# Sixteen expert products on one core: the up products split into two halves of 32 tokens, the second half behind a run-time branch

## The reference, cut to what matters

```python
scores = sigmoid(h @ w_router)
sel = scores + b_router
# the best of four groups of four experts, then the two best experts in it
_, idx = top_k(where(in_group, sel, -inf), 2)
for e in range(16):
    he = silu(h @ w1[e]) * (h @ w3[e])
    out = out + gates[:, e:e + 1] * (he @ w2[e])
```

## Time and profile before

| | us |
|---|---|
| median of 3 executions | 988.1 |
| lowest and highest | 986.34 and 995.4 |
| the profiled execution | 996.42 |
| its span in the trace | 994.6 |

### The profile page before, as it was taken

One profiled execution on the slowest core, in us unless ns is written; L12 is line 12 of the kernel. 1 busy time (PEld: TensorE's weight loads), 2 busy tenths in 40 slices (PEclk: granted clock), 3 DMA queues, 4 the chain that ended last, 5 costly groups with the idle time before them and its releaser, 6 DMA issues.

```text
span 994.6 us, 11764 instructions
## 1 busy us (share of the span) xinstructions
PE 936.2 (94%) x4268; PEld 513.5 (52%) x4269; DVE 416.4 (42%) x894; ACT 304.7 (31%) x693; POOL 31.4 (3%) x54
## 2 busy tenths in 40 slices
PE   3999999999998999987999999999989999999998
PEld 1464456565443344332455445455765546577763
DVE  1279597634461012421222322601956633336452
ACT  3200534232412213340322331312465632125420
POOL 0100200000000000000000002000000000000000
PEclk9999999999999999997999999999989999999999
DMA  9998614488559799898799999404227724423401
GB/s 350 362 386 316 141 58 173 161 318 320 204 222 337 239 360 387 299 392 318 278 396 393 397 378 307 154 31 159 87 86 252 224 74 169 169 88 111 130 13 42
DMA packets 105693, 230.74 MB, mean 232 GB/s; under 512 B 3125, under 2 KB 6505, under 8 KB 105497
## 3 DMA queue, kind: packets, MB, share of 16 engines
q1 hardware_dynamic: 100288, 217.85, 61.8%
q0 software_dynamic: 2208, 7.37, 2.6%
q10 hardware_dynamic: 3128, 4.62, 1.4%
HBM read 224.31 MB, written 5.51 MB: 231 GB/s over the span
## 4 chain that ended last, share of the span: by engine, by line
PE 78%; DVE 8%; DMA 6%; ACT 4%; issue 2%; SPq 1%; POOLq 1%; ACTq 0%; POOL 0%; DVEq 0%
PE bank L646 23%; PE bank L913 12%; PE bank L926 6%; PE bank L660 5%; DMA arena<-in_w_mod_dram 5%; PE bank L943 4%; PE bank L1221 3%; PE bank L1150 3%; PE bank L1240 2%; PE bank L1231 2%; PE bank L612 2%; DMA arena<-in_gla_w_in_dram 1%; PE bank L842 1%; PE bank L938 1%; PE bank L775 1%
## 5 line engine op out<-in xcount | busy, mean ns | idle before, releaser
L646 PE MATMUL bank<-arena 128*128 128x512 f32 (+3 forms) x592 | 238.0, 560 | 4.3 <-DMA arena<-in_gla_w_in_dram 2.3
L646 PEld LDWEIGHTS bank<-arena 128*128 128x128 f32 x592 | 111.8, 191 | 122.5 <-issue 110.4
L913 PE MATMUL bank<-arena 128*64 128x512 f32 x512 | 114.6, 600 | 2.9 <-issue 2.9
L660 PE MATMUL bank<-arena 128*128 128x256 f32 (+1 forms) x384 | 99.1, 416 | 2.8 <-ACT arena L1945 1.5
L660 PEld LDWEIGHTS bank<-arena 128*128 128x128 f32 x384 | 72.1, 190 | 30.6 <-issue 21.4
L913 PEld LDWEIGHTS bank<-arena 128*64 128x64 f32 x512 | 39.4, 139 | 74.5 <-issue 73.8
L926 PE MATMUL bank<-arena,con 128*64 128x512 f32 x272 | 67.7, 644 | 4.7 <-ACT con L1848 4.0
L2395 DVE TENSOR_TENSOR con<-con,bank 128x256 f32<-128x256 f32 x17 | 7.1, 420 | 111.1 <-ACT con L1753 111.1
L1749 ACT ACTIVATE con<-bank 128x256 f32<-128x256 f32 x17 | 6.5, 384 | 139.9 <-PE bank L913 139.9
L926 PEld LDWEIGHTS bank<-arena,con 128*64 128x64 f32 x272 | 22.3, 147 | 39.7 <-issue 38.6
L612 PE MATMUL bank<-arena,silu_c 128*32 128x512 f32 x272 | 35.9, 652 | 5.6 <-DMA arena<-in_w_mod_dram 4.1
(11 more groups left out here) (415 smaller groups left out, 1207.1 us busy)
## 6 DMA issues: line engine op xcount, KB each, us to landing
arena<-in_w_gate_e_dram SPq DMA_DIRECT2D x16, 2048.0 KB, 14.5
arena<-in_w_up_e_dram SPq DMA_DIRECT2D x16, 2048.0 KB, 13.2
arena<-in_w_down_e_dram SPq DMA_DIRECT2D x16, 2048.0 KB, 12.8
arena<-in_w_mod_dram SPq DMA_DIRECT2D x12, 2048.0 KB, 16.4
arena<-in_mod_w_dram SPq DMA_DIRECT2D x12, 2048.0 KB, 8.2
arena<-in_ab_w_in_dram SPq DMA_DIRECT2D x7, 2048.0 KB, 9.2
arena<-in_gla_w_in_dram SPq DMA_DIRECT2D x6, 2048.0 KB, 16.2
arena<-in_cd_w_in_dram SPq DMA_DIRECT2D x6, 2048.0 KB, 7.8
```

Of the source, the lines that this page charges most:

```text
L646: mm = pe.matmul(ps[:, 0:n], lhs[:, k, tile * P:(tile + 1) * P], w[:, k, c0:c0 + n], start=(k == 0), stop=(k == kd_ - 1))
L660: mm = pe.matmul(ps[:, i * n:(i + 1) * n], w[:, k, c * P:(c + 1) * P], rhs[:, k, 0:n], start=(k == 0), stop=(k == KC - 1))
L913: mm = pe.matmul(up_b[64 * j:64 * j + 64, :], h[:, k, :], blocks[:, g + n:u + n + 1:u - g, :], start=(k == 0), stop=(k == KC - 1), tile_po ...
```

## The change

- The up products of an expert are split by tokens (`up_half`). A half is 32 tokens: for each chunk k four matmuls with 32 stationary columns and 256 moving columns, each on its own 32 columns of the array (`tile_position=(0, 32 * j)`), with a quarter of the gate and of the up weights. The first half writes columns 0 to 255 of `up_b`, the second columns 256 to 511.
- DVE computes `passes`: 0 for up to 32 tokens, 1 for 33 to 64, 2 and more beyond, in four small linked steps and a copy, ahead of `extra_flag`.
- PE reads `passes` of the expert into a register. Above 0 it takes the wide branch: the loop of three surplus rounds, which now compares this register with the round's number, and then the second half. Otherwise it raises one semaphore. The first half is computed last, after the branch, in both cases. Expert 0 always computes both halves.
- `x_up`, `x_turned` and `x_down` become one semaphore, `x_step`, with three steps per round; an idle round raises it by 3 in one instruction without drains.
- ACT and DVE read and write the same number of elements as before, in another order (`ff_halves` and the views with `a` and `g`). `down` picks its columns of `ffT` accordingly.

Lines of the diff that only rename semaphores are left out:

```diff
@@ -216,6 +217,7 @@
         small = sb("small", [P, 1024 - 256 - 96])
         route_idx = sb("route_idx", [P, TT, 2], I32)
         extra_flag = sb("extra_flag", [P, NE, EXTRA], I32)
+        passes = small[:, 352:352 + NE].bitcast(I32)
         first_slot = small[:, 288:288 + NE * (1 + EXTRA)].rearrange("p (e t) -> p e t", t=1 + EXTRA).bitcast(I32)
 
         arena = sb("arena", [P, MAIN + 6 * SLOT])
@@ -223,6 +225,7 @@
         RING = MAIN + 3 * SLOT
         SPARE = KC * (2 * T + CAP)
         blocks = arena[:, :].rearrange("p (n c) -> p n c", c=256)
+        quarters = arena[:, :].rearrange("p (n c) -> p n c", c=P)
 
         def view(off, *dims):
             n = int(np.prod(dims))
@@ -273,6 +276,7 @@
         hs = [view(12800, KC, CAP), view(13312, KC, CAP)]
         spent = con[:, cols["levels"][0]:cols["levels"][0] + 768]
         act1, act2, ffT = spent[:, 0:256], spent[:, 256:512], spent[:, 512:768].rearrange("p (c s) -> p c s", c=2)
+        ff_halves = spent[:, 512:768].rearrange("p (q a s) -> p a q s", q=4, a=2)
...
@@ -523,6 +526,15 @@
                                                         sem("cdga_ready"))
         conv_in, cd_conv = sem("conv_in"), sem("cd_conv")
         sink_exp = sem("sink_exp")
+
+        def x_upped(n):
+            return n * 3 + 4
+
+        def x_turned(n):
+            return n * 3 + 5
+
+        def x_downed(n):
+            return n * 3 + 6
 
         block = ctx.enter_context(nc.Block())
 
@@ -903,27 +915,38 @@
             def landed_expert(e, j):
                 pe.wait_ge(landed[expert_slot[e][j]], 16 * expert_fill[e, j])
 
-            def up(h, e, sem_, gathered=False):
+            def up(h, e, sem_):
                 g, u = (slot_at(s) // 256 for s in expert_slot[e][0:2])
                 for k in range(KC):
-                    if gathered:
-                        pe.wait_ge((hg_a, hg_v)[k % 2], k // 2 + 1)
                     for j in range(2):
                         n = 2 * k + j
                         mm = pe.matmul(up_b[64 * j:64 * j + 64, :], h[:, k, :], blocks[:, g + n:u + n + 1:u - g, :],
                                        start=(k == 0), stop=(k == KC - 1), tile_position=(0, 64 * j))
                 mm.then_inc(sem_, 1)
 
+            def up_half(h, half, e, gathered=False):
+                g, u = (slot_at(s) // P for s in expert_slot[e][0:2])
+                for k in range(KC):
+                    if gathered:
+                        pe.wait_ge((hg_a, hg_v)[k % 2], k // 2 + 1)
+                    for j in range(4):
+                        n = 4 * k + j
+                        mm = pe.matmul(up_b[32 * j:32 * j + 32, 256 * half:256 * half + 256],
+                                       h[:, k, HALF * half:HALF * half + HALF], quarters[:, g + n:u + n + 1:u - g, :],
+                                       start=(k == 0), stop=(k == KC - 1), tile_position=(0, 32 * j))
+                return mm
+
             def turn_ff(sem_):
                 for c in range(2):
                     mm = pe.transpose(t_b[:, c * P:(c + 1) * P], act2[:, c * P:(c + 1) * P], ident)
                 mm.then_inc(sem_, 1)
 
-            def down(e, sem_):
+            def down(e, sem_, whole):
                 w2 = view(slot_at(expert_slot[e][2]), 4, D)
                 for kc in range(4):
+                    c, at = (kc // 2, 64 * (kc % 2)) if whole else (kc % 2, 64 * (kc // 2))
                     for q in range(2):
-                        mm = pe.matmul(dn_b[64 * q:64 * q + 64, :], ffT[:, kc % 2, 64 * (kc // 2):64 * (kc // 2) + 64],
+                        mm = pe.matmul(dn_b[64 * q:64 * q + 64, :], ffT[:, c, at:at + 64],
                                        w2[:, kc, 512 * q:512 * q + 512], start=(kc == 0), stop=(kc == 3),
                                        tile_position=(0, 64 * q))
                 mm.then_inc(sem_, 1)
@@ -950,30 +973,25 @@
                 project_gates(f"ga{n}", "ab4" if c else "ab3_ctx" if half else "ab3", [2 * i, 2 * i + 1], c == 1,
                               hT_ctx if half else hT_lat, ga_copied, n + 1)
 
-            pe.sem_inc(x_up, 1)
-            flags = extra_flag[0:1, :, :].rearrange("p e t -> p (e t)")
-
-            def extras(e):
+            pe.sem_inc(x_step, 3)
+
+            def extras(e, blocks_of_e):
                 with pe.Fori(0, EXTRA) as t:
-                    n = t + e * EXTRA
-                    flag = pe.value_load(flags[:, bass.ds(n, 1)], min_val=0, max_val=1)
-                    with pe.If(flag > 0):
+                    with pe.If(blocks_of_e > t + 1):
+                        n = t + e * EXTRA
                         pe.wait_ge(x_h, n + 1)
-                        up(hs_x, e, x_up)
+                        up(hs_x, e, x_step)
                         pe.wait_ge(x_ff, n + 1)
-                        turn_ff(x_turned)
+                        turn_ff(x_step)
                         landed_expert(e, 2)
                         pe.wait_ge(x_ffT, n + 1)
-                        down(e, x_down)
+                        down(e, x_step, False)
+                        pe.drain()
                     with pe.Else():
-                        pe.drain().then_inc(x_up, 1)
-                        pe.drain().then_inc(x_turned, 1)
-                        pe.drain().then_inc(x_down, 1)
+                        pe.sem_inc(x_step, 3)
 
             def no_extras():
-                pe.sem_inc(x_up, EXTRA)
-                pe.sem_inc(x_turned, EXTRA)
-                pe.sem_inc(x_down, EXTRA)
+                pe.sem_inc(x_step, 3 * EXTRA)
 
             def ctx_turned_latents(t):
                 pe.wait_ge(c_ready, t - 1)
@@ -1090,34 +1108,37 @@
                 ctx_work(CTX_WORK_TURNED.get(e, []))
                 landed_expert(e, 2)
                 pe.wait_ge(ffT_ready, e + 1)
-                down(e, down_done)
+                down(e, down_done, True)
 
             for e in range(NE):
                 for j in range(2):
                     landed_expert(e, j)
                 if e == 0:
-                    up(hg[:, :, 0:CAP], e, up_done, True)
-                any_extra = pe.value_load(flags[:, e * EXTRA:e * EXTRA + 1], min_val=0, max_val=1)
+                    up_half(hg, 1, e, True)
+                    up_half(hg, 0, e).then_inc(up_done, 1)
+                blocks_of_e = pe.value_load(passes[0:1, e:e + 1], min_val=0, max_val=1 + EXTRA)
                 if e == 0:
-                    with pe.If(any_extra > 0):
+                    with pe.If(blocks_of_e > 1):
                         ctx_latents(6)
                         gather()
                         behind_up(e)
-                        extras(e)
+                        extras(e, blocks_of_e)
                     with pe.Else():
                         no_extras()
                         c_place[0] -= 6
                         ctx_latents(6)
                         gather(True)
                         behind_up(e)
-                    pe.wait_ge(x_down, EXTRA)
+                    pe.wait_ge(x_step, x_downed(EXTRA - 1))
                     continue
-                with pe.If(any_extra > 0):
-                    extras(e)
+                with pe.If(blocks_of_e > 0):
+                    extras(e, blocks_of_e)
+                    pe.wait_ge(hs_ready, e)
+                    up_half(hs[e % 2], 1, e)
                 with pe.Else():
                     no_extras()
                 pe.wait_ge(hs_ready, e)
-                up(hs[e % 2], e, up_done)
+                up_half(hs[e % 2], 0, e).then_inc(up_done, 1)
                 behind_up(e)
                 ctx_work(CTX_WORK_BEHIND.get(e, []))
             for i in range(3):
@@ -1399,7 +1420,7 @@
                         banks.wait(sp, "qkT311")
                     sp.wait_ge(down_done if j0 == 2 else up_done, e0 + 1)
                     if e0 == 0:
-                        sp.wait_ge(x_down if j0 == 2 else x_up, EXTRA + (0 if j0 == 2 else 1))
+                        sp.wait_ge(x_step, x_downed(EXTRA - 1) if j0 == 2 else x_upped(EXTRA - 1))
                 elif s == 0:
                     banks.wait(sp, "y01")
                 elif s == 3:
...
@@ -1841,11 +1862,13 @@
                     act.wait_ge(hs_ready, e)
                     extras(e)
                 act.wait_ge(up_done, e + 1)
-                sigmoid(sig_step, 2 * e).then_inc(silu_done, 1)
+                sigmoid(sig_step, 2 * e, up_b[:, :].rearrange("p (a g c) -> p g a c", a=2, g=2)[:, 0],
+                        act1.rearrange("p (a c) -> p a c", a=2)).then_inc(silu_done, 1)
                 slot0 = slot_of(act, e * (1 + EXTRA))
                 ahead_of_turned(e)
                 act.wait_ge(ff_turned, e + 1)
-                act.activation(ffT, t_b[:, 0:256].rearrange("p (c s) -> p c s", c=2), ACT.Copy).then_inc(ffT_ready, 1)
+                act.activation(ff_halves, t_b[:, 0:256].rearrange("p (a q s) -> p a q s", a=2, q=4), ACT.Copy)\
+                   .then_inc(ffT_ready, 1)
                 behind_turned(e)
```

(41 more changed lines are left out.)

## The result

The changed kernel takes 998.25 us (median of 12 runs, 993.9 to 1002.0) against 990.41 us before (12 runs, 986.3 to 995.4): a ratio of 1.0082, 95% interval 1.0061 to 1.0103. It is 0.8% slower, where the prediction said 9 us faster.

What follows compares the result with a forecast made beforehand. PE was taken to lead the chain, with DMA close behind. Narrow-expert savings, less DVE, rounds and landing waits, left 11.3 us, taken as 9 for clock falls: 979 us from the median, range 970 to 996.

Steps and rivals of the forecast that it cites:

- The sum, followed through: Walk along experts 1 to 15 and on to `ab_gate`, with PE savings limited by weight landings: 11.3 us less.
- rival A2: Wide path's loops refetch instruction packets at 2.3 us per fetch; two such loops add 18 us: 997 us, chance 0.08.
- The half: Up products: 64 records in 3.5 us, saving 3.4 us per narrow expert, 30.3 us of PE time for nine.
- rival B: Up products: four column groups do not run together at 256 columns, each half takes 7 us: 1033 us, chance 0.05.
- Rival E: Fewer narrow experts than nine; excluded by counts, except expert 1 by rounding, costing 3 us; no chance of its own.
- Expert 0: DVE's four added steps and a copy delay expert 0, and everything behind until DMA leads, by 0.95 us.
- Rounds on the wide path: Three rounds walked by experts 5, 6, 7, 10 and 11: 0.8 us each, 2.4 us per expert, ends 0 and 3.9.
- Rival A: Wide path costs more than its rounds, deciding from about 5 us per wide expert; 995 us at 6; chance 0.08.
- Landings: DMA's weight landings make PE wait 5 to 7 us ahead of experts 5, 10 and 15.
- The clock: PE clock falls at waits before experts 5, 10 and 15: three cost 5.2 us; one or two assumed, leaving 9.
- the slow side: Whole kernel slower by more than the bound, beyond 998 us: B and half of A and A2, chance 0.13.

Runs made afterwards that it cites:

- skipped_code: Kernel before the change, with 128 more PE instructions that never run in each expert's branch for surplus rounds, behind a run-time condition: 1011.06 us, ratio 1.0208.
- loop_8_longer: loop_8 with 128 instructions that never run added to the wide branch of every expert but 8: 997.95 us, ratio 1.0071.
- apart: Changed kernel with surplus rounds and second half in two separate branches and the always-executed first half between them: 984.7 us, ratio 0.9934.
- apart_early: apart with the flag read and first branch ahead of the wait for the expert's gate and up weights: 981.51 us, ratio 0.9893.
- loop_8: Changed kernel with the loop of surplus rounds built for expert 8 alone, other experts raising the semaphore instead: 984.31 us, ratio 0.9911.
- static: Changed kernel with branches resolved at build time for these inputs, flag read and branch kept at experts 0 and 8 only: 976.16 us, ratio 0.9829.
- loop_wide: Changed kernel with the loop of surplus rounds kept only for experts 5, 6, 7, 8, 10 and 11: 987.76 us, ratio 0.9939.

## Why the prediction was wrong

**The step that failed is a term missing from "The sum, followed through": what a narrow expert pays for passing over the wide branch.** The sum gave these nine experts 3.4 us each and nothing else. The rival A2 named the mechanism, code that arrives late, but put it in the wrong place ("a loop that crosses from one packet's code into the next"), on the wide path, and gave it 0.08. The rows show it in the narrow jump and in the plain run right behind it: 20.0 us on the chain. Against the forecast the time is off by 998 - 979 = 19 us, of which 2.3 are the base (988.1 was the median of three runs, 990.4 that of twelve). Between the traces, from these context products at 278.48 (276.60 after) to `ab_gate` at 599.63 (602.65 after), the stretch grew by 4.9 us, where the sum had 11.3 less: 16.2 us. The 20.0 us cover that. That the rest of them fell where PE would have waited for weights in any case (see the landings below) is argued, not measured. skipped_code shows that the distance alone does this, loop_8_longer that it does so with no loop in it, apart that it goes when executed work stands between, with the same code fetched.

**The price of one fetch was too low.** A2 took 2.3 us from the shortest small transfer. The packet itself takes 1.1; with what lies ahead and behind, a branch took 5.1 to 7.0.

**How the rule was read.** The Trainium skill, "Runtime: NRT & Kernel Launch", section "Instruction fetch mechanics", says that a taken branch out of the current two pages of 256 instructions forces a fetch. I applied it to backward jumps of a loop. It says nothing of direction, and a jump of 260 instructions lands more than one page on: the trace agrees with it at three of the nine, with 5.1 to 7.0 us in place of 0.1 to 0.4. That five others took 0.42 us at most, and that 195 instructions already cost 4 to 6 us, fits too if what counts is where in its page the jump begins, but no run here moved that place by itself.

**The half was right.** 64 records in 3.59 us (forecast 3.5), wide 128 in 7.1: the row L612 was the right one, and rival B is out. Why L853 was slow no run shows. Rival E is out: 1472 records are those of the counts.

**Expert 0 was right.** Measured from the context products ahead of it (278.48 and 276.60), its up ended 1.2 us later (296.76 and 296.05), and PE stood idle 0.9 us for DVE's copy, where 0.95 was forecast.

**Rounds on the wide path: right in size.** Three rounds in the wide branch of expert 6 took 2.83 us by the sequencer's records (414.06 to 416.89); I took 2.4, ends 0 and 3.9. At expert 10 the last weights landed at 495.47 and the up started at 499.26, 3.8 us on, as forecast. Rival A, from 5 us on, is out: from the branch to the end of the rounds none of the five took over 3.0 us.

**Landings: right in kind where the fetches are away, wrong at expert 5.** In the kernel after DMA hardly got its lead before expert 15, since each lost microsecond of PE was passed on to the loads that wait for its ups: expert 15's weights landed at 581.9, not at 575.1. In apart_early they landed at 569.6, and PE waited 6.6 us for them, and 2.4 for expert 14's. The wait forecast at expert 5 did not come: in loop_8, static, apart and apart_early its last weights landed at 382.2 to 385.6 (386.1 forecast), just as PE came to it, and 0.4 us of idle at most stood out (in static); in loop_wide, with the rounds, it was 1.5. The clock was taken at 2 us; the estimate for it in the kernel after is 6. The sum of 11.3, of which 9 were left for the clock's sake, stands against 15.1 in static, which reads flags at experts 0 and 8 only, and 8.4 in the best general version.

**The chances.** The saving sits in exactly the nine experts that jump, and what they jump over had doubled. A2 named the longer wide branch as a risk, but for those who walk it; of the jump over it the prediction had no row, no bound and no rival. A rival with its place there (long jump, fetch, and PE's queue run dry behind it) should have stood in the list, with a price from zero to nine fetches, and the slow side would have had more than 0.13.

## What to carry to other kernels

Code that is skipped has a price: on an engine whose instructions stream in, count the instructions between a branch and its target, and keep executed work of a few microseconds between two bodies that are usually skipped, or decide at build time. If PE's row "issue" grows ahead of plain matmuls, lay the instruction queue's packets beside the gaps before looking at operands. And read flags and take branches ahead of a wait for data, where they are free, rather than behind it.

## What was not expected of the hardware

- A forward jump over some 260 instructions cost 5.1 to 7.0 us at three of nine places, 2.3 at one, and 0.4 at most at the others; over some 130 it cost 0.33 at most in the kernel before.
- Behind a jump that itself took 0.3 us the code can still run out: in skipped_code PE stopped for 3.75 us after 5 records of a product of 32, until 1.2 us behind a packet.
- 1,920 instructions that never run made a kernel 21 us slower, 2.1%, with 8 packets of 16 KB more.
- Four column groups at 256 columns run side by side as they do at 512: 16 rounds of four in 3.59 us, 0.22 us each.
